# A state-space scan on one core: a second place for broadcast decay rows, and a new order of the tile's steps

## The reference

```python
z, xbc, dt_f, dt_b, q, k, v, gates = split_cols(h @ w_in, IN_SPLITS)
xbc = silu(depthwise_centred_conv(xbc, conv_w, conv_b))          # 5 taps
xs, b_in, c_in = split_cols(xbc, ...)                            # 32 heads of 64; 4 groups of B and C
y = ssd_forward(xs, dt_f, a_f, B, C) + ssd_backward(xs, dt_b, a_b, B, C) + d_skip * xs
y = gated_group_rmsnorm(y, z, g)                                 # v = y*silu(z), normed over each group's 512 channels
branch_ssd = y @ w_br_ssd
out = (sigmoid(g_ssd) * branch_ssd + sigmoid(g_attn) * branch_attn) @ w_out
```

## Time and profile before

| | us |
|---|---|
| median of 3 runs (lowest, highest) | 2815.21 (2813.67, 2837.34) |
| the profiled execution | 2830.1 |
| its span, first to last instruction | 2828.4 |
| TensorE busy in the span | 2655.8 (94%) |
| VectorE busy | 1453.1 (51%) |
| ScalarE busy | 1245.2 (44%) |
| the scan stage (first product 1531.6 to first gate product 1873.6) | 342.0 |
| TensorE, VectorE, ScalarE busy in it | 298.2, 267.9, 267.0 |

### The profile page before, as it was taken

How to read it: one execution, slowest core, us unless ns; L and a number is a source line. 1 busy time by engine, 2 the same in 40 slices (tenths; PEclk the granted TensorE clock), 3 DMA queues, 4 the chain that set the end, 5 groups by cost and what they waited for, 6 DMA issues and landing times.

```text
span 2828.4 us, 52418 instructions
## 1 busy us (share of the span) xinstructions
PE 2655.8 (94%) x20916; PEld 2438.5 (86%) x20916; DVE 1453.1 (51%) x2514; ACT 1245.2 (44%) x2045; POOL 83.8 (3%) x157
## 2 busy tenths in 40 slices
PE   7998999999998699999989988889988998999998
PEld 7985899999996399999978776679966996899998
DVE  3233476553425766554467877762376344433333
ACT  3335354332425644432365777852465234333321
POOL 0000000000000000000001211200000000000000
PEclk9998999999999999999999999999999999999999
DMA  6420122223321022223353454532211231222232
GB/s 181 122 67 0 43 89 93 93 97 101 112 97 53 1 75 97 96 89 116 101 187 124 164 201 156 178 130 93 89 51 53 94 108 45 75 97 96 96 105 68
DMA packets 74693, 278.20 MB, mean 98 GB/s; under 512 B 9642, under 2 KB 9674, under 8 KB 74048
## 3 DMA queue, kind: packets, MB, share of 16 engines
q1 hardware_dynamic: 60816, 217.42, 22.9%
q0 software_dynamic: 13744, 58.88, 6.8%
HBM read 267.03 MB, written 9.24 MB: 98 GB/s over the span
## 4 chain that ended last, share of the span: by engine, by line
PE 78%; DVE 9%; ACT 5%; issue 4%; DMA 4%; DVEq 0%; ACTq 0%; POOL 0%; POOLq 0%; SPq 0%
PE acc L338 65%; PE acc L369 2%; DMA res_tmp<-scratch_rows 2%; PE ps L813 1%; DMA w_raw<-in_stream 1%; PE ps L369 1%; ACT w_hi L313 1%; DVE big L1602 1%; DVE w_lo L319 1%; PE ps L453 1%; DVE big L1276 1%; DVE big L2178 1%; PE acc L1467 1%; PE ps L802 1%; PE ps L1745 1%
## 5 line engine op out<-in xcount | busy, mean ns | idle before, releaser
L338 PE MATMUL acc<-x_split,w_hi 128*128 128x256 f32 x7968 | 1258.6, 280 | 17.7 <-DVE x_split L1363 12.0
L338 PEld LDWEIGHTS acc<-x_split,w_hi 128*128 128x128 f32 x7968 | 1076.0, 190 | 22.3 <-issue 16.2
L319 DVE TENSOR_TENSOR w_lo<-w_raw,w_hi 128x1024 fp32r<-128x1024 f32 x405 | 493.0, 1221 | 608.2 <-ACT w_hi L313 608.2
L338 PE MATMUL acc<-x_split,w_lo 128*128 128x256 f32 x3984 | 789.7, 280 | 0.0
L313 ACT ACTIVATE w_hi<-w_raw 128x1024 fp32r<-128x1024 f32 x405 | 424.8, 1054 | 578.6 <-PE acc L338 527.4
L338 PEld LDWEIGHTS acc<-x_split,w_lo 128*128 128x128 f32 x3984 | 610.0, 190 | 0.0
L338 PE MATMUL acc<-big_r,w_hi 128*128 128x256 f32 x3560 | 559.1, 279 | 7.7 <-DVE big_r L2231 3.4
L338 PEld LDWEIGHTS acc<-big_r,w_hi 128*128 128x128 f32 x3560 | 478.1, 189 | 9.8 <-issue 3.6
L338 PE MATMUL acc<-big_r,w_lo 128*128 128x256 f32 x1780 | 351.8, 279 | 0.0
L338 PEld LDWEIGHTS acc<-big_r,w_lo 128*128 128x128 f32 x1780 | 270.9, 189 | 0.0
L1847 ACT ACTIVATE res_tmp<-res_tmp 128x512 f32<-128x512 f32 (+3 forms) x256 | 121.1, 551 | 46.9 <-DVE res_tmp L1872 45.8
(11 more groups left out here) (291 smaller groups left out, 2583.3 us busy)
## 6 DMA issues: line engine op xcount, KB each, us to landing
w_raw<-in_stream SPq DMA_DIRECT2D x405, 512.0 KB, 3.3
res_tmp<-scratch_rows POOLq DMA_DIRECT2D x128, 320.0 KB, 6.0
scratch_bias<-res_tmp POOLq DMA_DIRECT2D x1, 2560.0 KB, 55.0
res_tmp<-in_x SPq DMA_DIRECT2D x2, 1024.0 KB, 7.7
res_tmp<-scratch_bias POOLq DMA_DIRECT2D x8, 256.0 KB, 4.4
scratch_x<-res_tmp POOLq DMA_DIRECT2D x1, 2048.0 KB, 9.0
scratch_kv<-big POOLq DMA_DIRECT2D x1, 2048.0 KB, 9.5
res_tmp<-scratch_x POOLq DMA_DIRECT2D x1, 2048.0 KB, 8.6
```

Source lines behind the costliest of these rows:

```text
L319: dve.tensor_tensor(w_lo[:, u.slot], w_raw[:, u.slot], w_hi[:, u.slot].bitcast(F32), ALU.subtract).then_inc(lo_done, 1)
L338: mm = pe.matmul(a[:, h], w, AR[:, x + k, h], start=(k == 0 and w is wh and x == hi and h.start == 0), stop=(k == total - 1 and w is wl), ...
```

## The change

All in the scan and its neighbour; the same arithmetic.

- Rows: chunks 0 and 1 of odd tiles get a place of their own (`both`): for tiles 1 to 9 slots 28 on and 44 on, which the scan's outputs of tiles 12 to 15 fill later, for tiles 11 to 15 the slots of B and C that are done with. So the transfers of chunks 0 and 1 wait for the heads two tiles back, those of chunks 2 and 3 still for the tile before. The 8 transfers of a tile keep their order in GpSimd's queue. Two heads' transfers share a semaphore.
- The weight stream has x's unit ahead of z's, so x is the first product tile; its convolution starts when that one is done.
- New orders on ScalarE and VectorE (in the diff). CB's chunk 3 uses bank 0 (bank 1 in group 0) instead of the bank of the transposes.
- All loops of the stage are written out.
- The first gate product of the next stage is put between the last transposes and the last heads.

```diff
+        ODD_EARLY, ODD_LATE = (VH + 12, 16), (BT, 4)
+        def both(f, c):
+            if f % 2 == 0 or c >= 2:
+                return A[:, ROWS:ROWS + 10].rearrange("p (b m) n -> p b (m n)", b=2), BACK[c]
+            first, apart = ODD_EARLY if f < 11 else ODD_LATE
+            return A[:, first:first + 2 * apart].rearrange("p (b m) n -> p b (m n)", b=2), BACK[c]
...
# ssd_rows_dma
-            def body(i):
+            for f in range(SSD_TILES):
                 for c in range(CH):
+                    before = f - 1 if c < 2 else f
                     for b in range(2):
-                        pool.wait_ge(ev("s_pv"), 8 * i + (2 * c + b + 1))
+                        if before >= 0:
+                            pool.wait_ge(ev("s_pv"), 8 * before + 2 * c + b + 1)
...
# ssd_pe
                     if c == 3 and not first:
-                        pe.wait_ge(ev("s_xtok"), 4 * g)
+                        pe.wait_ge(ev("s_v0"), 4 * g - 1)
...
-                    if j == 0:
-                        pe.wait_ge(ev("s_cb_rest"), 4 * g + 4)
...
+            product_tile(pe, Units(UB["br_ssd"]), Tiles(TB["br_ssd"]), XH, XL)
             heads(SSD_TILES - 1, 3)
             square_sum(GROUPS - 1)
...
# ssd_act, one tile (ux, tx are x's unit and tile; +1 are z's)
-                    tile_done(act, uz + 1)
+                    tile_done(act, ux)
...
-                    conv5_act(act, tz + 1, 8 + f, x)
-                    act.activation(A.at(VH, f), acc[tz.bank][:], ACT.Silu).then_inc(acc_free[tz.bank], 1)
-                    split_hi(act, uz + RING)
-                    split_hi(act, uz + 1 + RING)
+                    conv5_act(act, tx, 8 + f, x)
+                    split_hi(act, ux + RING)
+                    evacuated(act, tx)
+                    act.activation(x, x, ACT.Silu).then_inc(ev("s_xt"), 1)
+                    tile_done(act, ux + 1)
+                    act.activation(A[:, VH + f], acc[(tx + 1).bank][:], ACT.Silu).then_inc(acc_free[(tx + 1).bank], 1)
                     if j == 0:
                         table_rest(g)
-                    evacuated(act, tz + 1)
-                    act.activation(x, x, ACT.Silu).then_inc(ev("s_xt"), 1)
...
-                    act.wait_ge(ev("s_xtt"), f + 1)
-                    act.activation(A[:, XTOK + j % 2], ps[:, 2], ACT.Copy).then_inc(ev("s_xtok"), 1)
                     table_of_exp_and_ln(act)
...
                     for c in range(CH):
+                        if c == 2:
+                            act.wait_ge(ev("s_xtt"), f + 1)
+                            act.activation(A[:, XTOK + j % 2], ps[:, 2], ACT.Copy).then_inc(ev("s_xtok"), 1)
+                            split_hi(act, ux + 1 + RING)
                         act.wait_ge(ev("s_cap"), 4 * f + (c + 1))
...
# ssd_dve, one tile, all of the new order
+                    conv5_dve(dve, tx, f + 8, f + 8, A[:, XT + j % 2])
+                    cap(f, g * 8 + 2 * j, 0)
+                    cap(f, g * 8 + 2 * j, 1)
+                    split_lo(dve, ux + RING)
                     if j == 0:
                         table_diagonals(g)
...
                         dve.wait_ge(ev("s_cb"), 4 * g + 4)
                         dve.wait_ge(ev("s_cb_rest"), 4 * g + 4)
+                    times_cb(f, 0)
+                    if j or not first:
+                        out(f - 1, (j - 1) % 4)
+                    times_cb(f, 1)
+                    if j == 2 and not first:
+                        scaled(g - 1)
+                    cap(f, g * 8 + 2 * j, 2)
+                    cap(f, g * 8 + 2 * j, 3)
+                    split_lo(dve, ux + 1 + RING)
                     if j == 3 and not first:
-                        lows(g + (-1))
...
+                        lows(g - 1)
+                    times_cb(f, 2)
+                    times_cb(f, 3)
...
# gated_pe
-                product_tile(pe, u, t, XH, XL)
+                if j or stage != "br_ssd":
+                    product_tile(pe, u, t, XH, XL)
# the weight stream
-        unit_stack(interleave(z, xs, 1), (8,)),
+        unit_stack(interleave(xs, z, 1), (8,)),
```

More of the change, by code:

```diff
@@ L1567, in rows_buf, with part, back, fore @@
             return A[:, ROWS + 5 * b:ROWS + 5 * b + 5].rearrange("p b n -> p (b n)")
-        def part(b, c):
-            return rows_buf(b)[:, BACK[c]:BACK[c] + S + P]
+        def both(f, c):
[3 more added lines that the diff above has]
+            return A[:, first:first + 2 * apart].rearrange("p (b m) n -> p b (m n)", b=2), BACK[c]
+        def part(f, b, c):
+            rows, at = both(f, c)
+            return rows[:, b, at:at + S + P]
+        def back(f, b, c):
+            return part(f, b, c)[:, 0:LENB[c]]
+        def fore(f, b, c):
+            return part(f, b, c)[:, LENB[c]:S + P]
         cb_packed = A[:, CB:CB + 5].rearrange("p b n -> p (b n)")
@@ L1775, in group @@
                     mm.then_inc(ev("s_xtt"), 1)
-            group(0, True)
-            with pe.Fori(1, GROUPS) as g:
-                group(g)
+            for g in range(GROUPS):
+                group(g, g == 0)
+            product_tile(pe, Units(UB["br_ssd"]), Tiles(TB["br_ssd"]), XH, XL)
             heads(SSD_TILES - 1, 3)
@@ L1845, in group @@
                                 head = g * 8 + (2 * j + b + 32 * k)
-                                x = w[:, at:at + n]
-                                ins = act.activation(x, x, ACT.Exp, bias=tab[:, 0, c, ds(head, 1)])
+                                ins = act.activation(w, w, ACT.Exp, bias=tab[:, 0, c, head:head + 1])
                             ins.then_inc(ev("s_e"), 1)
             act.activation(A[:, BG], A[:, BT], ACT.Copy).then_inc(ev("s_bg"), 1)
-            group(0, True)
-            with act.Fori(1, GROUPS) as g:
-                group(g)
+            for g in range(GROUPS):
+                group(g, g == 0)
@@ L1863, in cap @@
             def cap(f, head, c):
-                for b in range(2):
-                    dve.wait_ge(ev(f"s_row_in{b}{c}"), 16 * (f + 1))
-                x = A[:, ROWS:ROWS + 10].rearrange("p (b m) n -> p b (m n)", b=2)
-                x = x[:, :, (S + 2 * P) * c:(S + 2 * P) * c + 2 * P].rearrange("p b (k n) -> p b k n", k=2)
+                dve.wait_ge(ev(row_in(f, c)), 32 * (f // 2 + 1 if c < 2 else f + 1))
+                rows, at = both(f, c)
+                x = rows[:, :, at + c * P:at + c * P + 2 * P].rearrange("p b (k n) -> p b k n", k=2)
                 own = tab[:, 1, c].rearrange("p (k h) -> p h k", k=2)
@@ L1872, in cap, with times_cb @@
                 dve.tensor_tensor(x, x, own, ALU.min).then_inc(ev("s_cap"), 1)
[L1874 to L1877 removed]
+            def times_cb(f, c):
+                for b in range(2):
+                    dve.wait_ge(ev("s_e"), 8 * f + (2 * c + b + 1))
+                    w, cb = part(f, b, c), cb_packed[:, BACK[c]:BACK[c] + S + P]
+                    dve.tensor_tensor(w, w, cb, ALU.mult).then_inc(ev("s_w"), 1)
             def out(f, j):
```

67 lines of the change are left out of this document (24 added, 43 removed).

## The result

The changed kernel takes 2809.2 us (median of 20 runs), the kernel before 2834.1 beside it: a ratio of 0.993, 95% interval 0.990 to 0.995. In a second series the two were 2802.4 (10 runs) and 2828.2 (33 runs), 0.992 (0.988 to 0.995). So it is faster by 0.7 to 0.8%, about 21 to 24 us by the ratios, 24.9 and 25.8 by the medians. I had forecast 25.6 us less and 2790 us, with a range of 2777 to 2807. The gain by the medians is about the one forecast, the time is not, and lies 2 us above my range: the level that I started from, 2815.2 from three runs, was low.

The account below looks back on a forecast made before the run. No engine is full; the order of the work bounds the scan. Start 2.15, groups 7.8, 2.2, 4.9 and 3.0 (20.1 together) plus gate 5.5 give 25.6 us off 2815.2: 2790, range 2777 to 2807.

Parts of the forecast that it names:

- The tile's walk: Scan: a plain tile, from s, the start of VectorE's convolution, takes 16.4 us; groups 68.3, 79.7, 79.7 and 79.35.
- the tiles with extras: Scan, a full group's tiles with their extra work: 21.7, 18.1, 19.0 and 20.9 us, convolution to convolution.
- The table load: ScalarE in a scan tile: the load of 1.28 us goes ahead of the wait, under the convolution.
- rival A: ScalarE in the scan: table load behind the wait, plain tiles 17.7 us, taking 15.7 of the gain, 2805; chance 0.13.
- Chunks 2 and 3 in tile 1: Scan: heads release these rows about 2.1 us after the convolution starts, four transfers take 8.8; no wait counted.
- rival B: Scan: rows of chunks 2 and 3 late; each us costs one in 15 tiles; at 2.7, 2830; chance 0.07.
- The gate's tile: Scan's end: the gate's first product tile fills TensorE's idle 8.38 us before the last heads; gain 5.5 us.
- The start: First group: first convolution at about 1541.5 instead of 1543.65, needing only the first product tile; gain 2.15 us.
- The level: Whole kernel: the profiled execution gives 2804.5; the median 2815.2 is 0.5% lower and gives 2789.6.
- C: Scan: TensorE becomes the bound if other waits overlap better; three groups give 19 us more, 2771; chance 0.09.
- D: Scan: the change does nothing, row waits replaced in full and the gate's gain lost; chance 0.01.

Follow-up runs that it names:

- f3: The changed kernel with a second, already fulfilled wait ahead of the convolution's wait at the Silu of x; 0.997 of the kernel before.
- e3: The changed kernel with tile 1's square sum put behind heads and transposes, rstd behind the exponentials of chunks 0 and 1; 0.993 of the kernel before.
- e0: The changed kernel run again without any edit, as the base for the runs beside it; 0.992 of the kernel before.
- f1: The kernel before, in its old order, with only the gate's first product tile put in front of the last heads; 0.997 of the kernel before.
- e2: The changed kernel with the gate's first product tile put back behind the square sums; 0.997 of the kernel before.
- g1: f4 with chunk 2's rows of tiles up to 10 also fetched a tile early; 0.981 of the kernel before.
- e1: The changed kernel with its new order but the second home for rows taken away; 1.006 of the kernel before.
- f4: The changed kernel with diagonals, scaled, lows and squares moved into idle gaps, plus the two moves of e3; 0.982 of the kernel before.
- g0: f4 run again unchanged, as the base for the runs beside it; 0.987 of the kernel before.
- g2: The changed kernel with only VectorE's three moves (CB's diagonals behind the convolution, scaled and lows before the exponentials); 0.990 of the kernel before.

## Why the prediction was right or wrong

**The tile's walk: right.** s+6.60, 8.25, 11.83, 16.4, and the tiles with extras, 21.7, 19.0 and 20.9, are read as 21.7, 19.0 and 20.9. VectorE's waits for rows went from 34.8 to 8.1 us, and its waits for the exponentials rose from 5.9 to 36.2 (19.2 and 17.0). That is why so little is left of 35 us.

**The table load: right.** It starts directly behind split_hi, ahead of the wait, 16 times. With two waits in a row it starts behind them (f3, 16 times), as it did at 1879.37. So both rows agree with what f3 shows. The Trainium skill's sentence (ScalarE: Activation LUTs, Step-by-step: what each stage is for), that the load is placed right before its activation, leaves open on which side of the waits; the trace shows that a single wait stands behind the load. (The prediction calls this reading "the second rival below"; it is rival A, the first.)

**Chunks 2 and 3 in tile 1: the step that failed in the sum.** I put the release of chunk 2 at "about s+2.1" for every tile, bounded the lateness by 0.9 us and took 0. That holds in a plain tile (s+1.5 to 2.6 in tiles 1 to 3), but in tile 1 of a group the square sum stands ahead of the heads that release the rows, and the prediction has no term for it. In tile 9 the square sum begins with the first square, after 4.16 us of idle time, and ran at a granted clock of 0.70; the heads start at s+3.0. Chunk 2 was issued at s+5.2, 6.7 and 8.0 in tiles 5, 9 and 13. Its four transfers took 7.6 to 9.8 us to the last landing, around the 8.8 that I had, so it is the release that was wrong. Cap 3 started at s+15.0, 16.5 and 15.6; by the walk it asks at 13.0 (11.7 and the 1.27 of rstd). Tiles 5, 9 and 13 took 19.7, 21.2 and 20.3 instead of 18.1, 18.1 and 17.7, together 7.4 us, and that is all of the difference in groups 1 to 3 (79.7, 79.7, 79.35 against 81.3, 82.8, 82.0: 7.4). It is rival B's mechanism, in three tiles instead of fifteen. e3 takes it out of tile 1 and brings half of it back in tile 2, as the release times say.

**The gate's tile: right in place, 2 us too large at first.** 5.5 forecast, 3.5 in the first profile (10.47 to 6.94), 4.9 in e0, 6.1 alone (f1). The differences go with the granted clock of the last heads and the square sum: 0.50 and 0.82 in the first profile, 0.60 and 1.00 in e0, 1.00 and 1.00 in f1. The prediction priced TensorE's work there at the full clock.

**The start: right.** From the last matmuls ahead of the scan (1531.0 before, 1525.9 after) to the first convolution 12.6 us become 10.4; 2.15 was forecast.

Together: start 2.2, groups 10.5, gate 3.5, 16.2 us where 25.6 were forecast. By the second profile 18.7. Held against f1's groups, which are in before's order, the groups gain 7.4 and 8.5 us instead of 10.5 and 11.6, so the stage's gain is known to some 3 us. The measured ratios, 21 and 24 us, have intervals of 8 and 9 us to each side, and hold the traces' 16 to 19 as well as the forecast 25.6. That the medians agree with the forecast is then partly luck.

**The level: the step that put the time out of the range.** I went from the profiled execution to the median of three runs, 2815.2, as if that were known to 0.1%. The kernel before had medians of 2834 (20 runs, those three among them), 2828 (33), 2818 (29) and 2827 (11), the last three each on another chip, and its runs lie between 2800 and 2859. From 2834.1 the forecast would have been 2808.5, against 2809.2, and from 2828.2 it would have been 2802.6, against 2802.4. So the starting level was 19 us low, and the range of 2777 to 2807 had no term for it.

One source of the spread is in the traces, outside the scan. In the second up projection, whose code is the same in all kernels, TensorE is without idle time, and 255 us hold these matmuls before, after, and in the changed kernel's second profile (columns: stretch, length, busy time and number, granted clock, transfers' share, GB/s):

Before:

```profile
1065.00:1320.00 255.00, 255.00 (x2167) 1.00 0.30 99
```

After:

```profile
1065.00:1320.00 255.00, 254.93 (x2249) 1.00 0.31 104
```

After, e0:

```profile
1065.00:1320.00 255.00, 254.94 (x2167) 1.00 0.31 101
```

2249 in one execution and 2167 in two others, 3.6% fewer, at a granted clock of 1.00 each time: a matmul every 113.5 or every 117.8 ns. In the 13 profiles of the study five have the slow pace there and eight the fast one, whatever the kernel. It is worth 10 us in this one stretch. The pace changes within an execution: from 2500 to 2740 us e0, e2, e3 and f3 have the slow one (2040 matmuls) and the other nine the fast one (2120 or 2121), the kernel before among them. The two first profiles differ by 26.9 us in span: 16.2 are the scan's, 5.1 come before it and 5.6 after it, in code that is the same. What sets the pace stays open; no run here was made for it.

**The rivals.** A is what f3 is: true where the program has two waits. B holds in tile 1 of a group. C did not come: TensorE's bound shows only in g1, where it is busy for 72.1 of 72.1 and 71.2 of 72.2 us. D fell: the stage is shorter, and both intervals of the ratio end below 1.

## What to carry to other kernels

When a transfer is hidden by a second buffer, the work that covered it before is free to move, and has to be moved: here the order without the home was a loss (e1; the home in the old order was not tried), and the order's own gaps were worth another 0.5 to 1% (f4, g0, g1). Walk one period of the loop with spacings from the trace, engine by engine; in the changed kernel it was good to 0.1 us in all tiles but those where rows came late. Ask for every buffer when it is released in the tile with the most work ahead of the release, and not only in the plain one. Take the level from many runs, and the gain from the trace of the stretch that was changed.

## What the runs showed of the hardware

In the scan a table load goes ahead of a single wait, and behind the waits where there are two: an added wait that was always fulfilled took group 0 from 68.3 to 72.4 us (f3).

After 4.16 us of idle time TensorE's next 5.3 us were granted 0.70 of the clock, after 4.92 us the next 4.6 us 0.50, that is the lower of its two levels, 1.2 GHz, for all of it. The length of the last gap does not tell it alone: at the scan's end, behind the gate's product and 1.98 to 2.00 us of idle time, the same 16 matmuls of the heads were granted 0.58 in e0, 0.63 in g2, 0.73 in f4 and 1.00 in g0, and took 4.04, 3.83, 3.61 and 2.71 us.

Four row transfers of 320 KB, issued back to back, took 7.4 to 9.8 us from the first issue to the last landing in the changed kernel (chunks 2 and 3).

Four taps of the convolution on VectorE took 3.43 us in the hardware loop and 3.11 written out.

The same matmuls ran at two paces 3.8% apart, one every 113.5 or every 117.8 ns, at the same granted clock of 1.00, in stretches of some hundred microseconds.
